# Stick-breaking attention on one core: masked entries zeroed by position on GpSimd, and the next pair's scores issued a pair ahead

## The chip, the cores and the metric

The kernel runs on 1 core of one Trainium2 chip. The metric is device time in microseconds (us) of one execution; lower is better. Engines are named as in the profile: PE is TensorE's matmul, PEld its weight load, DVE is VectorE, ACT is ScalarE, POOL is GpSimd, SP is SyncE.

## The reference

The program is a trunk of four residual layers over 256 tokens of width 1024. Layers 0 and 3 mix tokens by stick-breaking attention, layer 1 by latent attention, layer 2 by windowed attention; a SwiGLU block follows each. The change touches only stick-breaking, with 16 heads of 64:

```python
z = jnp.einsum('bqhd,bshd->bhqs', q_blk, k) * scale
valid = key_pos[None, :] < q_pos[:, None]
log_keep = jnp.where(valid, jax.nn.log_sigmoid(-z), 0.0)
log_keep_after = lax.cumsum(log_keep, axis=3, reverse=True) - log_keep
att = jnp.where(valid, jnp.exp(log_beta + log_keep_after), 0.0)
return jnp.einsum('bhqs,bshd->bqhd', att, v)
```

With softplus(z) = max(z, 0) + ln(1 + exp(-|z|)), log_keep is -softplus(z), and the exponent is z minus the sum of softplus over this key and all later valid keys. An entry is valid when its key comes before its query.

## The kernel before

Every engine has its own program, written out by hand in order, and engines meet at semaphores. Matrices are held as a high and a low part (float32r), so each product is three matmuls: high by high, high by low, low by high. The layer's 16 projection weights (units b to b+15, 128x2048 each) stream in by DMA; for each unit ACT makes the high part w_hi (L503, in `split`) and DVE the low part w_lo (L862, in `split`, counted by lo_done), some units ahead of PE's use.

Heads go in eight pairs p. `qk(p)` on PE projects a pair's queries and keys (24 matmuls for four of its eight k-tiles, so two halves); DVE scales them out of PSUM (L972, L974), ACT makes their high parts k_hi and q_hi (L565, L567), DVE the low parts (`qk_low`: L981, L985). `logits(p)` computes transposed scores, keys on partitions and queries on columns, into two PSUM banks: "early" are keys 0 to 127 for all queries of both heads (512 columns), "late" keys 128 to 255 for queries 128 to 255 (256 columns). Before the scores, two bf16 matmuls of an identity with a mask write -1e30 at the masked entries (L1459, L1461). ACT does |z|, exp and ln on the 768 columns (`soft`: L579, L581, L583); DVE adds max(z, 0) twice, into sp_hi and into a scratch buffer (L998), and sp_lo is their difference (L1003). `keep_sums(p)` accumulates minus the sums of softplus onto the scores (L1487 to L1489, waiting for softplus and then for sp_lo). ACT's exp (`weights`, L588) makes the attention weights, and `values(p)` (L1410, L1412) multiplies them with v. ACT and DVE split the result for the output projection (L592 o_hi, L948 o_lo).

In loop step p PE issues logits(p), the values of finished pairs (two pairs in steps 2, 4 and 6, one in step 7), the second half of qk(p+1) and the first of qk(p+2), then keep_sums(p). In steps 6 and 7 parts of the output projection stand in place of qk: `out_part(i, j, tiles)` needs o_lo of each of its tiles, and w_lo of unit b+12+j for its first tile. sp_hi and sp_lo (`soft_split`) exist once, not per pair; so do k_split and q_split. The scores of pair p lie in bank pair p mod 2.

Of the kernel before, what the change touches and what calls it, by code (L numbers as in the profile page):

```python
# [22 lines left out]
FP32 = mybir.dt.float32  # L23
# [6 lines left out]
P = 128  # L30
# [76 lines left out]
def trunk(nc, w, x_in, consts, gains, bv, final_rows, rel_rows, rel_scratch, out):  # L107
    ctx = ExitStack()
    with ctx:
# [29 lines left out]
        q_split = placed("q_split", [P, 2, 2, SEQ], FP32R, 4 * KT * SEQ)  # L139
# [95 lines left out]
        def head_blocks(v):  # L235
            return v.rearrange("p (h b q) -> p h b q", h=2, b=2)
# [54 lines left out]
        def signals(tag, names):  # L291
# [8 lines left out]
            signals("m0", "v_new qk_new q_zero k_hi q_hi k_lo q_lo z ln softplus sp_lo sums att av o_hi o_lo"),  # L300
# [4 lines left out]
            signals("m3", "v_new qk_new q_zero k_hi q_hi k_lo q_lo z ln softplus sp_lo sums att av o_hi o_lo"),  # L305
# [41 lines left out]
        def _(pool):  # L347
# [84 lines left out]
            def query_zeros(i):  # L432
# [6 lines left out]
                for h in range(2):  # L439
                    if h:  # L440
                        pool.wait_ge(mixer[i].q_zero, 1)
                    pool.memset(q_split[others(h), :, h, :].bitcast(FP32), 0.0).then_inc(mixer[i].q_zero, 1)
                pool.wait_ge(mixer[i].q_zero, 2)

# [23 lines left out]
            for i in range(DEPTH):  # L468
# [5 lines left out]
                if i % 3 == 0:  # L474
                    query_zeros(i)
                if i == 1:
# [10 lines left out]
        def _(act):  # L487
# [57 lines left out]
            def stick_breaking(i):  # L545
# [17 lines left out]
                def qk_hi(p):  # L563
                    act.wait_ge(m.qk_new, 2 * p + 2)
                    act.activation(k_split[:, 0, :], k_all[:, p, :], ACT.Copy).then_inc(m.k_hi, 1)  # L565
                    for h in range(2):
                        act.activation(q_split[own(h), 0, h, :], q_all[own(h), p, :], ACT.Copy).then_inc(m.q_hi, 1)  # L567
# [7 lines left out]
                def soft(p):  # L575

                    e, z = buf(0, 768), two_banks[p % 2][:, 0:768]
                    act.wait_ge(m.z, p + 1)
                    t = step(act.activation(e, z, ACT.Abs))  # L579
# [5 lines left out]
                def weights(p):  # L585

                    act.wait_ge(m.sums, p + 1)
                    act.activation(buf(2 + p % 2, 768), two_banks[p % 2][:, 0:768], ACT.Exp).then_inc(m.att, 1)  # L588
# [258 lines left out]
        def _(dve):  # L847
# [102 lines left out]
            def stick_breaking(i):  # L950
# [28 lines left out]
                def qk_low(p):  # L979
# [3 lines left out]
                    for h in range(2):  # L983
                        dve.wait_ge(m.q_hi, 2 * p + h + 1)
                        dve.tensor_tensor(q_split[own(h), 1, h, :], q_all[own(h), p, :],  # L985
                                          q_split[own(h), 0, h, :].bitcast(FP32), ALU.subtract).then_inc(m.q_lo, 1)
# [3 lines left out]
                if i == 0:  # L990

                    dve.wait_ge(lut_summed, 1)
                    dve.tensor_copy(rel_lut[:, :], bank[7][0:16, 0:192]).then_inc(lut_copied, 1)
                for p in range(KT):
                    split(b + 7 + p)
                    dve.wait_ge(m.ln, p + 1)
# [1034 lines left out]
```

## Time and profile before

| What | Value |
|---|---|
| Median of 3 runs | 1161.99 us (1161.47 to 1162.59) |
| Profiled execution, its own time | 1161.93 us |
| Span of the profiled execution | 1160.1 us |
| PE busy | 1148.3 us, 99% of the span |
| DVE, ACT, POOL busy | 804.5, 633.8, 276.0 us |
| Granted TensorE clock, mean | 0.998 |
| Loop over eight pairs, layer 0 and layer 3 | from 41 to 111 us and from 882 to 952 us |

The span is the stretch that the profiler sees; the execution's own time is 1.83 us longer. An engine's busy time is the union of its instructions' times; matmuls overlap one another, so the distance from one start to the next is what one costs in a dense run.

### The profile page before, as it was taken

The numbers are of one execution on the slowest core, as the hardware profiler recorded it, in microseconds if no ns is written. First come the engines' busy times: TensorE is split into PE (matmuls) and PEld (weight loads), VectorE is DVE, ScalarE is ACT, GpSimd is POOL, SyncE is SP. The second block draws the span as 40 slices with busy tenths as digits, with TensorE's granted clock in tenths as the row PEclk, the third lists the DMA queues.
The fourth block names the chain that finished last, engine by engine and source line by source line (L and its number), as shares of the span: only waits on it lengthen the run. The fifth ranks groups of instructions, "written<-read, shape, count | busy, mean of one in ns | idle before, by whom it ended". The sixth has DMA issues, their size and how long they took to land.

```text
span 1160.1 us, 17714 instructions
## 1 busy us (share of the span) xinstructions
PE 1148.3 (99%) x7182; PEld 1020.4 (88%) x7182; DVE 804.5 (69%) x881; ACT 633.8 (55%) x753; POOL 276.0 (24%) x257
## 2 busy tenths in 40 slices
PE   9999999999999999999999999999999999999997
PEld 7899888888998888888899888888889998888885
DVE  6786877776588677777658777777546868777742
ACT  6776565564445556555346656555436765655632
POOL 2100533231123444221111343221110005332100
PEclk9999999999999999999999999999999999999999
DMA  9432555565563255555554355555555326555550
GB/s 350 166 110 73 218 189 195 197 199 191 186 208 111 97 191 185 182 187 196 197 182 146 110 181 188 197 195 182 183 184 178 110 73 219 190 197 195 197 184 37
DMA packets 31227, 201.75 MB, mean 174 GB/s; under 512 B 3648, under 2 KB 4736, under 8 KB 7728
## 3 DMA queue, kind: packets, MB, share of 16 engines
q1 hardware_dynamic: 28800, 196.88, 47.9%
q10 hardware_dynamic: 2032, 3.07, 1.0%
q8 instruction: 57, 0.93, 0.3%
q0 software_dynamic: 320, 0.72, 0.3%
q14 instruction: 18, 0.15, 0.0%
HBM read 198.43 MB, written 1.25 MB: 172 GB/s over the span
## 4 chain that ended last, share of the span: by engine, by line
PE 94%; DVE 2%; POOL 1%; DMA 1%; SPq 1%; issue 1%; ACT 1%; ACTq 0%; DVEq 0%; POOLq 0%
PE banks L1338 41%; PE banks L1342 21%; PE banks L1326 8%; PE banks L1332 6%; PE banks L1334 6%; PE banks L1333 6%; PE banks L1473 1%; DMA raw<-w 1%; PE banks L1410 1%; PE banks L1487 1%; PE banks L1629 1%; PE banks L1475 0%; SPq L320 0%; PE banks L1641 0%; POOL scratch L360 0%
## 5 line engine op out<-in xcount | busy, mean ns | idle before, releaser
L862 DVE TENSOR_TENSOR w_lo<-raw,w_hi 128x2048 fp32r<-128x2048 f32 x180 | 442.7, 2464 | 191.8 <-ACT w_hi L503 191.6
L503 ACT ACTIVATE w_hi<-raw 128x2048 fp32r<-128x2048 f32 x183 | 348.6, 1907 | 61.6 <-PE banks L1326 21.1
L1338 PE MATMUL banks<-x_split,w_hi 128*128 128x512 f32 x1408 | 336.9, 391 | 0.0
L1338 PEld LDWEIGHTS banks<-x_split,w_hi 128*128 128x128 f32 x1408 | 258.4, 188 | 50.3 <-DVE w_lo L862 0.4
L1342 PEld LDWEIGHTS banks<-x_split,w_lo 128*128 128x128 f32 x1408 | 181.0, 191 | 7.1
L1342 PE MATMUL banks<-x_split,w_lo 128*128 128x256 f32 x1408 | 184.0, 283 | 0.0
L1338 PE MATMUL banks<-hid_split,w_hi 128*128 128x512 f32 x528 | 129.9, 391 | 0.0
L1338 PEld LDWEIGHTS banks<-hid_split,w_hi 128*128 128x128 f32 x528 | 95.6, 188 | 17.5
L1332 PE MATMUL banks<-x_split,w_hi 128*128 128x256 f32 x384 | 110.0, 286 | 0.0
L1333 PE MATMUL banks<-x_split,w_hi 128*128 128x256 f32 x384 | 108.6, 283 | 0.0
L1334 PE MATMUL banks<-x_split,w_lo 128*128 128x256 f32 x384 | 108.6, 283 | 0.0
L395 POOL TENSOR_TENSOR scratch<-scratch,rstd 128x512 f32<-128x512 f32 x44 | 57.2, 1300 | 196.1 <-ACT scratch L788 196.1
L398 POOL TENSOR_TENSOR scratch<-scratch 128x512 f32<-128x512 f32 x44 | 72.2, 1642 | 126.9 <-DVE scratch L1250 126.2
L515 ACT ACTIVATE x_split<-x,vec 128x256 fp32r<-128x256 f32 x64 | 31.6, 506 | 107.5 <-DVE x L1285 81.4
L776 ACT ACTIVATE scratch<-banks 128x512 f32<-128x512 f32 x44 | 26.2, 595 | 95.1 <-PE banks L1342 95.1
L1332 PEld LDWEIGHTS banks<-x_split,w_hi 128*128 128x128 f32 x384 | 73.4, 191 | 2.2 <-issue 1.0
L383 POOL TENSOR_TENSOR sq<-x 128x256 f32<-128x256 f32 x41 | 42.9, 1047 | 133.0 <-DVE x_split L887 131.8
L1342 PEld LDWEIGHTS banks<-hid_split,w_lo 128*128 128x128 f32 x528 | 70.5, 191 | 4.4
L1333 PEld LDWEIGHTS banks<-x_split,w_hi 128*128 128x128 f32 x384 | 73.5, 191 | 0.1
L1334 PEld LDWEIGHTS banks<-x_split,w_lo 128*128 128x128 f32 x384 | 73.5, 191 | 0.0
L1342 PE MATMUL banks<-hid_split,w_lo 128*128 128x256 f32 x528 | 71.7, 282 | 0.0
L383 POOL TENSOR_TENSOR sq_sum<-x 128x256 f32<-128x256 f32 x7 | 7.1, 1009 | 240.2 <-DVE x_split L887 240.2
(200 smaller groups left out, 1628.7 us busy)
## 6 DMA issues: line engine op xcount, KB each, us to landing
raw<-w SPq DMA_DIRECT2D x183, 1024.0 KB, 4.9
raw<-w SPq DMA_DIRECT2D x8, 256.0 KB, 6.4
x<-x_in SPq DMA_DIRECT2D x4, 256.0 KB, 5.3
raw<-w SPq DMA_DIRECT2D x2, 512.0 KB, 7.5
k_all<-k_all ACTq DMA_DIRECT2D x1, 960.0 KB, 8.0
rel_bias<-rel_scratch POOLq DMA_DIRECT2D x8, 64.0 KB, 3.0
y_gain<-final_rows ACTq DMA_DIRECT2D x1, 512.0 KB, 6.3
out<-y_rows SPq DMA_DIRECT2D x2, 256.0 KB, 2.6
```

The costliest lines, as they stand in the source:

```text
L383: step(pool.tensor_tensor(dst[:, :], x[:, k, :], x[:, k, :], ALU.mult))
L395: pool.tensor_tensor(gate, gate, both(rstd[:, 0:SEQ]), ALU.mult).then_inc(f.scaled, 1)
L398: pool.tensor_tensor(value, gate, value, ALU.mult).then_inc(f.hid, 1)
L503: act.activation(w_hi[u % HI_SLOTS][:, :], raw[slot][:, :], ACT.Copy).then_inc(hi_done, 1)
L515: act.activation(x_hi[:, k, :], x[:, k, :], ACT.Identity, scale=gain(n, k)).then_inc(norm.hi, 1)
L862: dve.tensor_tensor(w_lo[slot][:, :], raw[slot][:, :], w_hi[u % HI_SLOTS][:, :].bitcast(FP32), ALU.subtract).then_inc(lo_done, 1)
L1326: ins = pe.matmul(dst, a, v, start=first and n == 0, stop=last and n == 2, skip_group_check=True)
L1332: pe.matmul(dst, wh, xh, start=first, stop=False, skip_group_check=True)
L1333: pe.matmul(dst, wh, xl, start=False, stop=False, skip_group_check=True)
L1334: return pe.matmul(dst, wl, xh, start=False, stop=last, skip_group_check=True)
L1338: return pe.matmul(pair(b), wt[0], xs, start=first, stop=False, skip_group_check=True)
L1342: return pe.matmul(pair(b)[:, 1, :], wt[1], xs[:, 0, :], start=False, stop=last, skip_group_check=True)
```

## The change

The mask matmuls go, and the scores start their own accumulation. In their place POOL gets three instructions for each pair (`stick_masks`, L448): it writes zero at masked entries of the scratch copy of softplus and of sp_hi before they are summed (signal sp_kept), and of the attention weights before `values` (signal att_kept). An affine_select compares an index worked out from partition and column with zero and keeps or replaces the entry. So that one instruction reaches all four diagonal blocks, columns are laid out anew: late first (256 columns), then early by query block and head; q_split gets the same order.

PE's order changes too. logits(p+1) stands ahead of keep_sums(p), behind the first half of qk(p+2); it waits until `weights` of the pair two back has read its banks. The parts of the output projection in steps 5 to 7 are distributed anew. DVE and ACT follow with `softplus(p+1)`, `softplus_low(p+1)` and `soft(p+1)` in step p. Since sp_hi exists once, its second writing waits for the sums of the pair before.

```diff
+            def later_keys_out(v):
+                return pool.affine_select(v[:, 0:512], v[:, 0:512], [[0, 4], [1, P]], ALU.is_gt, 0.0, base=0,
+                                          channel_multiplier=-1)
+            def stick_masks(i):
+                def kept_softplus(p):
+                    pool.wait_ge(m.softplus, 2 * p + 1)
+                    later_keys_out(buf(1, 768)).then_inc(m.sp_kept, 1)
+                    pool.wait_ge(m.softplus, 2 * p + 2)
+                    later_keys_out(soft_split[:, 0, :]).then_inc(m.sp_kept, 1)
+                kept_softplus(0)
+                for p in range(KT):
+                    if p < KT - 1:
+                        kept_softplus(p + 1)
+                    pool.wait_ge(m.att, p + 1)
+                    later_keys_out(buf(2 + p % 2, 768)).then_inc(m.att_kept, 1)
...
+                soft(0)
+                qk_hi(1)
                 for p in range(KT):
-                    soft(p)
                     if p < KT - 1:
+                        soft(p + 1)
                         split(b + 8 + p)
-                        qk_hi(p + 1)
+                    if p < KT - 2:
+                        qk_hi(p + 2)
                     for done in finished(p):
                         out_hi(done)
                     weights(p)
...
+                def softplus(p):
+                    dve.wait_ge(m.ln, p + 1)
+                    for dst in (buf(1, 768), sp_hi):
+                        if p:
+                            dve.wait_ge(m.sums if dst is sp_hi else m.sp_lo, p)
+                        dve.scalar_tensor_tensor(dst, stick_scores(p), 0.0, buf(0, 768),
+                                                 ALU.max, ALU.add).then_inc(m.softplus, 1)
+                def softplus_low(p):
+                    dve.wait_ge(m.sp_kept, 2 * p + 2)
+                    dve.tensor_tensor(sp_lo, buf(1, 768), sp_hi.bitcast(FP32), ALU.subtract).then_inc(m.sp_lo, 1)
...
                 for p in range(KT):
                     split(b + 7 + p)
+                    if p < KT - 2:
+                        qk(p + 2)
+                    if p < KT - 1:
+                        softplus(p + 1)
+                    if p < KT - 2:
+                        qk_low(p + 2)
+                    if p < KT - 1:
+                        softplus_low(p + 1)
                     for done in finished(p):
                         dve.wait_ge(m.o_hi, done + 1)
                         out_lo(m, o_lo[:, done, :], bank[6 + done % 2][:, 0:SEQ], o_hi[:, done, :])
...
-                    mask = head_blocks(mask_b[:, 0:512])[:, :, 0, :]
-                    pe.matmul(head_blocks(early)[:, :, 0, :], ident_b[:, :], mask, start=True, stop=False,
-                              skip_group_check=True)
-                    pe.matmul(late, ident_b[:, :], mask, start=True, stop=False, skip_group_check=True)
+                    if p < 2:
+                        pe.wait_ge(m.v_new, 2 * p + 2)
+                    else:
+                        pe.wait_ge(m.att, p - 1)
...
+                logits(0)
+                qk(1, range(4, KT))
+                qk(2, range(0, 4))
                 for p in range(KT):
+                    if p < KT - 1:
+                        logits(p + 1)
+                    if p < KT - 2:
+                        qk(p + 2, range(4, KT))
+                    elif p == KT - 2:
+                        out_part(i, 1, range(0, 4))
+                    else:
+                        out_part(i, 0, range(4, 6))
+                        out_part(i, 1, range(4, 5))
                     for done in finished(p):
                         values(done)
+                    keep_sums(p)
+                    if p < KT - 3:
+                        qk(p + 3, range(0, 4))
+                    elif p == KT - 3:
                         out_part(i, 0, range(0, 4))
```

The changed program's line numbers differ: softplus is L1029, softplus_low L1034, qk_low L1010 and L1014, w_lo L891, o_lo L977, the sums L1533 to L1535, the scores L1519 and L1521. Three places show the new order.

First, DVE in layer 0 from step 6 on, where w_lo_57 is unit b+13 and w_lo_58 is b+14. Before:

```order
L862 TENSOR_TENSOR w_lo_57<-raw_52,w_hi 128x2048 [waits hi_done]
L998 SCALAR_TENSOR_TENSOR soft_split<-banks,scratch 128x768 [waits ln_m0]
L998 SCALAR_TENSOR_TENSOR scratch<-banks,scratch 128x768
L972 SCALAR_TENSOR_TENSOR q_all<-banks,rstd 128x256 [waits unit_used]
L974 TENSOR_TENSOR k_all<-banks,rstd 128x256
L1003 TENSOR_TENSOR soft_split<-scratch,soft_split 128x768 [waits softplus_m0]
L981 TENSOR_TENSOR k_split<-k_all,k_split 128x256 [waits k_hi_m0]
L985 TENSOR_TENSOR q_split<-q_all,q_split 64x256 [waits q_hi_m0] x2
L948 TENSOR_TENSOR o_split<-banks,o_split 128x256 [waits o_hi_m0] x2
L862 TENSOR_TENSOR w_lo_58<-raw_53,w_hi 128x2048 [waits hi_done]
```

Of the change, from the second softplus of step 5 on:

```order
L1029 SCALAR_TENSOR_TENSOR soft_split<-banks,scratch 128x768 [waits sums_m0]
L1010 TENSOR_TENSOR k_split<-k_all,k_split 128x256 [waits k_hi_m0]
L1014 TENSOR_TENSOR q_split<-q_all,q_split 64x2x128 [waits q_hi_m0] x2
L1034 TENSOR_TENSOR soft_split<-scratch,soft_split 128x768 [waits sp_kept_m0]
L891 TENSOR_TENSOR w_lo_57<-raw_52,w_hi 128x2048 [waits hi_done]
L1029 SCALAR_TENSOR_TENSOR scratch<-banks,scratch 128x768 [waits sp_lo_m0,ln_m0]
L1029 SCALAR_TENSOR_TENSOR soft_split<-banks,scratch 128x768 [waits sums_m0]
L1034 TENSOR_TENSOR soft_split<-scratch,soft_split 128x768 [waits sp_kept_m0]
L977 TENSOR_TENSOR o_split<-banks,o_split 128x256 [waits o_hi_m0] x2
L891 TENSOR_TENSOR w_lo_58<-raw_53,w_hi 128x2048 [waits hi_done]
```

The low parts o_lo of pairs 4 and 5 (L977) now stand behind a softplus that waits for PE's sums of pair 6, and behind a subtraction that waits for POOL.

Second, PE at the end of step 6, the sums of pair 6 and what follows. Before, the masks and scores of pair 7 follow:

```order
L1487 MATMUL banks<-soft_split,neg_sums 128x512 [waits sp_lo_m0]
L1488 MATMUL banks<-soft_split,neg_sums 128x256
L1489 MATMUL banks<-soft_split,neg_sums 128x2x128
L1459 MATMUL banks<-mask_b,ident_b 128x2x128
L1461 MATMUL banks<-mask_b,ident_b 128x256
L1473 MATMUL banks<-q_split,k_split 128x512 [waits k_hi_m0,q_hi_m0]
```

Of the change, where the scores of pair 7 have gone ahead, the output projection of tile 4 follows at once:

```order
L1533 MATMUL banks<-soft_split,neg_sums 128x512 [waits sp_lo_m0]
L1534 MATMUL banks<-soft_split,neg_sums 128x256
L1535 MATMUL banks<-soft_split,neg_sums 128x256
L1376 MATMUL banks<-o_split,w_hi 128x256 [waits o_lo_m0]
L1377 MATMUL banks<-o_split,w_hi 128x256
L1378 MATMUL banks<-o_split,w_lo_56 128x256
```

Its first matmul waits for o_lo of pair 4, which the DVE rows above place behind those same sums.

Third, POOL behind its two memsets of q_split in layer 0. Before, the squares for the next norm follow:

```order
L442 MEMSET q_split 64x2x256 [waits cast_done,ss_norm]
L442 MEMSET q_split 64x2x256 [waits q_zero_m0]
L383 TENSOR_TENSOR sq_sum<-x 128x256 [waits lo_norm,q_zero_m0]
L383 TENSOR_TENSOR sq<-x 128x256 [waits lo_norm,pool_step]
L387 TENSOR_TENSOR sq_sum<-sq_sum,sq 128x256 [waits pool_step]
```

Of the change:

```order
L443 MEMSET q_split 64x4x128 [waits cast_done,ss_norm]
L443 MEMSET q_split 64x4x128 [waits q_zero_m0]
L448 AFFINE_SELECT scratch<-scratch 128x512 [waits softplus_m0,q_zero_m0]
L448 AFFINE_SELECT soft_split<-soft_split 128x512 [waits softplus_m0]
L448 AFFINE_SELECT scratch<-scratch 128x512 [waits softplus_m0]
L448 AFFINE_SELECT soft_split<-soft_split 128x512 [waits softplus_m0]
L448 AFFINE_SELECT scratch<-scratch 128x512 [waits att_m0]
```

24 such instructions in each of the two layers now stand between the memsets and the squares.

## Rows read from the trace of the kernel before

**Rows 1.** The page: busy time of each engine, share of the span, instructions.

```profile
PE 1148.3 (99%) x7182; PEld 1020.4 (88%) x7182; DVE 804.5 (69%) x881; ACT 633.8 (55%) x753; POOL 276.0 (24%) x257
```

**Rows 2.** Waits of PE, longest: waited for, us, times, longest.

```profile
PE banks L1368 <- POOL ss L361: 1.4, 1, 1.4
```

**Rows 3.** Timeline of PE, layer 0, steps 0 and 1: start us, us, instruction.

```profile
48.64 0.48 PE L1487 MATMUL banks<-soft_split,neg_sums 128*128 128x512 f32 x1
48.97 0.28 PE L1488 MATMUL banks<-soft_split,neg_sums 128*128 128x256 f32 x1
...
49.20 0.28 PE L1459 MATMUL banks<-mask_b,ident_b 128*128 128x256 bf16 x1
...
49.79 0.40 PE L1473 MATMUL banks<-q_split,k_split 128*128 128x512 f32 x1
50.02 0.28 PE L1475 MATMUL banks<-q_split,k_split 128*128 128x256 f32 x1
```

**Rows 4.** Timeline of PE, end of the last sums of layer 0.

```profile
110.59 0.28 PE L1489 MATMUL banks<-soft_split,neg_sums 128*128 128x256 f32 x1
110.70 0.28 PE L1332 MATMUL banks<-o_split,w_hi 128*128 128x256 f32 x1
```

**Rows 5.** Timeline of ACT: step 4 of layer 0, and the last weights.

```profile
76.49 0.81 ACT L579 ACTIVATE scratch<-banks 128x768 f32<-128x768 f32 x1 [0.47 <-PE banks L1475]
...
78.96 1.90 ACT L503 ACTIVATE w_hi<-raw 128x2048 fp32r<-128x2048 f32 x1
81.86 0.42 ACT L565 ACTIVATE k_split<-k_all 128x256 fp32r<-128x256 f32 x1 [0.99 <-DVE k_all L974]
...
110.91 0.81 ACT L588 ACTIVATE scratch<-banks 128x768 f32<-128x768 f32 x1 [4.13 <-PE banks L1489]
```

**Rows 6.** Timeline of DVE: step 4 of layer 0, and one o_lo.

```profile
75.54 2.29 DVE L862 TENSOR_TENSOR w_lo<-raw,w_hi 128x2048 fp32r<-128x2048 f32 x1
79.09 0.96 DVE L998 SCALAR_TENSOR_TENSOR soft_split<-banks,scratch 128x768 fp32r<-128x768 f32 x1 [1.26 <-ACT scratch L583]
...
81.07 0.42 DVE L972 SCALAR_TENSOR_TENSOR q_all<-banks,rstd 128x256 f32<-128x256 f32 x1 [0.16 <-PE banks L1334]
...
81.74 0.95 DVE L1003 TENSOR_TENSOR soft_split<-scratch,soft_split 128x768 fp32r<-128x768 f32 x1
82.61 0.42 DVE L981 TENSOR_TENSOR k_split<-k_all,k_split 128x256 fp32r<-128x256 f32 x1
82.94 0.86 DVE L985 TENSOR_TENSOR q_split<-q_all,q_split 64x256 fp32r<-64x256 f32 x2
...
109.27 0.42 DVE L948 TENSOR_TENSOR o_split<-banks,o_split 128x256 fp32r<-128x256 f32 x1
```

**Rows 7.** Groups by line and shape, POOL: busy us, mean ns of one.

```profile
L452 POOL TENSOR_TENSOR scratch<-scratch,small 128x512 f32<-128x512 f32 x8 | 8.3, 1041 | 43.4 <-DVE small L1178 43.4
...
L367 POOL CAST mask_b<-scratch 128x832 bf16<-128x832 f32 x1 | 0.9, 872 | 0.0
L365 POOL CAST ident_b<-table 128x128 bf16<-128x128 f32 x1 | 0.3, 287 | 0.0
```

**Rows 8.** Timeline of POOL, squares after layer 0, and a product in the SwiGLU block.

```profile
120.95 2.54 POOL L383 TENSOR_TENSOR sq<-x 128x256 f32<-128x256 f32 x1
...
126.02 0.61 POOL L383 TENSOR_TENSOR sq<-x 128x256 f32<-128x256 f32 x1
...
185.09 1.29 POOL L398 TENSOR_TENSOR scratch<-scratch 128x512 f32<-128x512 f32 x1 [3.50 <-DVE scratch L1250]
```

**Rows 9.** Timeline of DVE at the same two places.

```profile
120.32 2.70 DVE L862 TENSOR_TENSOR w_lo<-raw,w_hi 128x2048 fp32r<-128x2048 f32 x1
...
185.50 3.02 DVE L862 TENSOR_TENSOR w_lo<-raw,w_hi 128x2048 fp32r<-128x2048 f32 x1 [0.56 <-ACT w_hi L503]
```

**Rows 10.** Stretches at the end: busy us (count) of PE, PEld, DVE, ACT, POOL, PEclk, DMA.

```profile
1152.00:1154.00 2.00, 0.47 (x3) 0.04 (x1) 0.75 (x1) 1.48 (x4) 0.00 (x0) 1.00 0.18 68
1154.00:1156.00 2.00, 0.00 (x0) 0.00 (x0) 1.32 (x7) 0.92 (x4) 0.00 (x0) 0.76 0.52 195
```

More of the change, by code:

```diff
@@ L299, in trunk @@
         mixer = [
-            signals("m0", "v_new qk_new q_zero k_hi q_hi k_lo q_lo z ln softplus sp_lo sums att av o_hi o_lo"),
+            signals("m0", "v_new qk_new q_zero k_hi q_hi k_lo q_lo z ln softplus sp_kept sp_lo sums att att_kept av o_hi o_lo"),
             signals("m1", "q_part q_new rope_tab rot_in krope_sum krope_new kfill k_part k_new v_part v_new logits max_new "
@@ L304, in trunk @@
                           "o_hi o_lo"),
-            signals("m3", "v_new qk_new q_zero k_hi q_hi k_lo q_lo z ln softplus sp_lo sums att av o_hi o_lo"),
+            signals("m3", "v_new qk_new q_zero k_hi q_hi k_lo q_lo z ln softplus sp_kept sp_lo sums att att_kept av o_hi o_lo"),
         ]
@@ L475, in _ @@
                     query_zeros(i)
+                    stick_masks(i)
                 if i == 1:
@@ L566, in qk_hi @@
                     for h in range(2):
-                        act.activation(q_split[own(h), 0, h, :], q_all[own(h), p, :], ACT.Copy).then_inc(m.q_hi, 1)
+                        act.activation(q_split[own(h), 0, :, h, :], q_all[own(h), p, :].rearrange("p (b q) -> p b q", b=2),
+                                       ACT.Copy).then_inc(m.q_hi, 1)
                 qk_hi(0)
@@ L587, in weights @@
                     act.wait_ge(m.sums, p + 1)
-                    act.activation(buf(2 + p % 2, 768), two_banks[p % 2][:, 0:768], ACT.Exp).then_inc(m.att, 1)
+                    act.activation(buf(2 + p % 2, 768), stick_scores(p), ACT.Exp).then_inc(m.att, 1)
                 def out_hi(p):
@@ L1471, in logits @@
                             pe.wait_ge(m.k_hi, p + 1)
-                        kk, qq = k_split[:, key_low, :], q_split[:, query_low, :, :]
-                        pe.matmul(early, kk[:, 0:P], qq.rearrange("p h s -> p (h s)"), start=False, stop=query_low == 1,
+                        kk, qq = k_split[:, key_low, :], q_split[:, query_low, :, :, :]
+                        first = not (key_low or query_low)
+                        pe.matmul(early, kk[:, 0:P], qq.rearrange("p b h q -> p (b h q)"), start=first, stop=query_low == 1,
                                   skip_group_check=True)
-                        last = pe.matmul(late, kk[:, P:SEQ], qq[:, :, P:SEQ], start=False, stop=query_low == 1,
-                                         skip_group_check=True)
+                        last = pe.matmul(late, kk[:, P:SEQ], qq[:, 1, :, :].rearrange("p h q -> p (h q)"), start=first,
+                                         stop=query_low == 1, skip_group_check=True)
                     last.then_inc(m.z, 1)
@@ L1483, in keep_sums @@
                         pe.wait_ge(neg_tri_done, 1)
-                    for low, done, count in ((0, m.softplus, 2 * p + 2), (1, m.sp_lo, p + 1)):
+                    for low, done, count in ((0, m.sp_kept, 2 * p + 2), (1, m.sp_lo, p + 1)):
                         pe.wait_ge(done, count)
                         sp = soft_split[:, low, :]
-                        pe.matmul(early, neg_tri, sp[:, 0:512], start=False, stop=False, skip_group_check=True)
-                        pe.matmul(late, neg_tri, sp[:, 512:768], start=False, stop=low == 1, skip_group_check=True)
-                        last = pe.matmul(head_blocks(early)[:, :, 1, :], neg_one, sp[:, 512:768], start=False,
+                        pe.matmul(early, neg_tri, sp[:, 256:768], start=False, stop=False, skip_group_check=True)
+                        pe.matmul(late, neg_tri, sp[:, 0:256], start=False, stop=low == 1, skip_group_check=True)
+                        last = pe.matmul(early[:, 256:512], neg_one, sp[:, 0:256], start=False,
                                          stop=low == 1, skip_group_check=True)
```

54 lines of the change are left out of this document (21 added, 33 removed).

## The prediction

> **What bounds the kernel now.** The page comes first: PE is busy 99% of the span, DVE 69%, ACT 55%, POOL 24% [rows 1]. So time is won only where PE has less to issue or waits less, and any new wait of PE costs its full length unless a wait already there swallows it. The waits of PE come next: the longest in the whole span is 1.4 us, near the start, outside the attention loop [rows 2]. The timeline of PE then gives the price of everything in the loop: a 256-column matmul starts 0.12 us after the one before [rows 4], a 512-column one takes 0.23 [rows 3]. One small wait recurs: the second L1487 starts its successor 0.33 later instead of 0.23, because sp_lo is just late [rows 3]. That is 0.10 us, in the four pairs per layer (0, 1, 3, 5) whose steps have no values to cover it.
>
> **What the change takes away.** The two masks and the first pair of score matmuls take 49.20 to 49.79, 0.59 us, of which the scores are 0.23 + 0.12 [rows 3, 4]; the masks are 0.24. Eight pairs give 1.92 us in each layer. The four sp_lo waits go as well, since a pair's scores now run a whole step ahead of its sums: 0.40. Gain: 2.3 us per layer, 4.6 in all. The new columns change no size of a PE instruction, so they are costed at nothing.
>
> **What it adds on PE's path.** A step without values takes PE 1.05 (three score groups of 0.35) + 48 x 0.12 + 0.94 (sums) = 7.75 us. I follow DVE from the moment at which PE has issued the last of sums(p-1), t = 0. An engine sees PE's signal 0.21 us after issue [rows 4, 5]; I take 0.1 between other engines and 0.15 to PE, estimates of the same order. DVE's occupancies are 0.67 for scaling a pair's q and k, 0.87 for each softplus and for sp_lo, 0.33 for k_lo, 0.43 for each half of q_lo, 2.29 for w_lo [rows 6].
>
> A select's own price is not in the trace. The nearest rows are one-input POOL casts: 128 columns take 0.287 us and 832 take 0.872, so 512 come to 0.61 [rows 7]. A product of the same 512 columns with two inputs takes 1.04, my upper bound; the lower one is 0.50, a little under the cast line. I take 0.65.
>
> The trace also shows that POOL and DVE take turns. A POOL square of 0.61 us took 2.54 when it began during a w_lo, and a w_lo of 2.29 took 3.02 when it began 0.41 us into a POOL product of 1.29 [rows 6, 8, 9]. Both instructions read two SBUF tensors there. On the other side 0.61 is unhindered beside DVE work out of PSUM [rows 8]. So k_lo, q_lo, sp_lo and w_lo should take turns with the selects, softplus should not. The Trainium skill (GPSIMD Engine Reference, Key points) says that GpSimd shares its SBUF interfaces with VectorE and contends with instructions of two SBUF inputs; the rows agree, and by that sentence the selects meet those four DVE instructions. Whether a one-input select also holds DVE up no row shows; I take that it does, for 0.5 us (0.65 less what POOL spends before it reads, about 0.15: the square above ended 0.47 after w_lo did, against 0.61 alone).
>
> Then, in a step whose predecessor had no values: qk(p+1) ended 0.94 before t = 0, so DVE scales it from -0.73 to -0.06, writes the first softplus to 0.82, the second to 1.70 (it needs the sums, there at 0.21), k_lo to 2.03. Now the select of sp_hi holds it to 2.53, half of q_lo to 2.96, the select of the weights to 3.46, the other half to 3.89; PE sees q_lo at 4.05. PE wants it behind 24 projections and two score groups, at 2.88 + 0.70 = 3.58. **PE waits 0.47**, in scores 2, 3, 5 and 7: 1.9 us. After a step with values DVE has done its first softplus early and is in time.
>
> **Scores 1**: measured from the end of scores 0, DVE gets qk(1) at 2.88 + 0.21, and does the scaling (3.76), two softplus (5.51), k_lo (5.84), a select's turn (6.34) and q_lo (7.20). PE wants q_lo at 5.76 + 0.70 = 6.46 and sees it at 7.35: 0.9 us.
>
> **Step 6, unit b+13.** From t = 0 at the sums of pair 5, DVE has q_lo at 3.89, sp_lo at 4.77, and only then does the w_lo that the moved `out_part(i, 1, ...)` needs: 7.06, at PE 7.2. PE stands there at 3.58 + 0.47 + 0.35 = 4.4. It waits 2.8 us. Before, that projection came a step later.
>
> **Step 7, o_lo.** This is the largest. Behind the sums of pair 6 PE has nothing to issue but `out_part(i, 0, range(4, 6))`, which needs o_lo of pair 4. On DVE that stands behind the softplus of pair 7, whose second half needs those very sums: 0.21 + 0.95 + 0.1 + 0.65 (select) + 0.1 + 0.87 (sp_lo) + 0.42 (o_lo) + 0.15 = 3.45 us of idle PE.
>
> **Values 7.** Exp and select now follow the last sums: 0.21 + 0.81 + 0.1 + 0.65 + 0.15 = 1.92 us [rows 5], against 12 projections, 1.44: 0.5. Without a select it was 1.17, and covered.
>
> ACT is tight but in time. From the scores' end its chain is 0.21 + 2.5 for the three passes (76.49 to 78.96), 1.9 for w_hi, 1.2 for k_hi and two halves of q_hi (three of 0.4), 0.81 for the weights that free the banks, 0.15 to PE; with 1.05 for the scores that is 7.8 against 7.75 [rows 5]. I count nothing: a wait of 0.1 would run beside the one for q_lo.
>
> **Sum.** Per layer 1.9 + 0.9 + 2.8 + 3.45 + 0.5 = 9.5, less 2.3, is +7.2 us; two layers +14.4. The profiled execution's own time is 1161.93 (span 1160.1 and 1.83 around it), the median 1161.99, so no shift is needed: **1176.3 us**.
>
> **Rivals.** *POOL gives way*: a one-input select waits for DVE but never holds it. Then scores 2 to 7 don't wait, scores 1 wait 0.4, w_lo of b+13 comes at 6.8 for a PE at 3.93 (2.9), the rest stays: 7.2 - 2.3 = 4.9 per layer, 1171.7 us. Without any meeting of the two, w_lo comes at 6.2, 2.3 late: 1170.5. For it: no row has a one-input POOL instruction first; against it: the w_lo of 3.02.
>
> *Slow selects*: at 1.04 us each turn is 0.9, and the first select ends 0.3 after DVE wants k_lo. The four waits of 0.47 become 1.6, scores 4 and 6 wait 0.6, scores 1 1.4, step 7 and the last values 0.4 more each: 16.5 - 2.3 = 14.2 per layer, about 1190 us. The skill's page above (Performance pitfalls) gives 1.03 to 2.03 cycles an element for a compare and select, at 1.2 GHz 0.44 to 0.87 us; by 0.87 the sum would be an estimated 1185, by 0.44 about 1171.
>
> *Faster*: if DVE reached w_lo of b+13 and o_lo of pair 4 before PE needs them, only the gain of 4.6 would be left, 1157.3 us. This is decided at 2.3 us of waits per layer; step 7 alone, without its select, is 2.8. It takes a DVE order other than the one shown, or hand-overs far shorter than the 0.21 seen. *No change*: waits that happen to sum to 2.3 per layer, 1162.
>
> *The clock*: PE's last stretch with matmuls ends within 1152 to 1154, and the mean granted clock of 1154 to 1156 is 0.76, on its way from 2.4 to 1.2 GHz [rows 10]; the idle of 1.4 us in [rows 2] left the mean at 0.998. An idle of 3.45 us may therefore drop it. Matmuls then take twice the time for a while, an estimated 1 to 3 us per layer. It comes on top of the first three; I leave it out of the forecast and in the range.
>
> **How the numbers follow.** Turns with selects near 0.65: 45%. POOL gives way or no meeting: 25%. Slow selects: 17%. Faster: 8%. Within 0.2%, about what a measurement of this kernel can tell from no change: 3%. Slower still: 2%. The range runs from 1167 (shorter selects, no turns, with 1 us per layer less of tail) to 1192 (slow selects with some clock lost), leaving out the faster and equal cases and the dearest end. Faster 0.08, same 0.03, slower 0.89.
>
> **What would show it.** L1459 and L1461 gone, PE's count down by 32 matmuls. PE idle after L1535 of pair 6 by 3 to 4 us, ended by DVE's o_lo (L977), in both layers; before the `out_part` of step 6 by 2 to 3 us, ended by w_lo (L891). Affine selects of about 0.65 us, and q_lo stretched where one runs beside it. Wrong would be: no idle at those two places, selects over 1 us (dearer), or scores that wait for `weights` (ACT) instead of q_lo.

## The result, and the profile after

The changed kernel takes 1179.38 us (median of 4, 1178.64 to 1180.87) against 1162.29 us (1161.47 to 1163.25) for the kernel before on the same chip: a ratio of 1.0149, 95% interval 1.0137 to 1.0161, so 1.5% slower. The forecast was 1176.3 us, in a range from 1167 to 1192. The profiled execution took 1180.87 us, its span is 1179.1 us, and the mean granted clock 0.991 where it had been 0.998.

The page's row of busy times and the clock's row of 40 slices, to lay beside [rows 1]. The last line is the clock's row of the kernel before:

```profile
PE 1153.7 (98%) x7150; PEld 1024.6 (87%) x7150; DVE 814.8 (69%) x881; ACT 631.9 (54%) x753; POOL 308.6 (26%) x305
...
PEclk9998999999999999999999999999999989999999
...
PEclk9999999999999999999999999999999999999999
```

PE has 32 matmuls fewer: the masks are gone. POOL has 48 instructions more. PE is nevertheless busy 5 us longer, and the clock row has an 8 in the two slices in which the attention loops end. The waits of PE in the changed kernel (waited for, total us, times, longest), to lay beside [rows 2]:

```profile
PE banks L1376 <- DVE o_split L977: 7.0, 2, 3.5
PE banks L1376 <- DVE w_lo L891: 5.2, 2, 2.6
...
PE banks L1519 <- DVE q_split L1014: 1.1, 2, 0.5
...
PE banks L1454 <- POOL scratch L448: 0.5, 2, 0.3
```

All four are new, each twice: once per layer. The two on top are o_lo of pair 4 (step 7) and w_lo of unit b+13 (step 6). Because the ends of matmuls overlap, I read the length of an idle from starts: the distance from one matmul's start to the next, less what the first one costs. PE's timeline in layer 0 shows scores 1, scores 2, the two idles, and the last values:

```profile
48.22 0.28 PE L1521 MATMUL banks<-q_split,k_split 128*128 128x256 f32 x1
49.04 0.50 PE L1519 MATMUL banks<-q_split,k_split 128*128 128x512 f32 x1 [0.54 <-DVE q_split L1014]
49.38 0.28 PE L1521 MATMUL banks<-q_split,k_split 128*128 128x256 f32 x1
...
56.77 0.28 PE L1521 MATMUL banks<-q_split,k_split 128*128 128x256 f32 x1
56.99 0.50 PE L1519 MATMUL banks<-q_split,k_split 128*128 128x512 f32 x1
...
100.07 0.28 PE L1521 MATMUL banks<-q_split,k_split 128*128 128x256 f32 x1
102.93 0.58 PE L1376 MATMUL banks<-o_split,w_hi 128*128 128x256 f32 x1 [2.58 <-DVE w_lo L891]
...
107.38 0.44 PE L1454 MATMUL banks<-scratch,v_all 128*64 128x256 f32 x2
...
109.80 0.28 PE L1535 MATMUL banks<-soft_split,neg_sums 128*128 128x256 f32 x1
113.57 0.58 PE L1376 MATMUL banks<-o_split,w_hi 128*128 128x256 f32 x1 [3.48 <-DVE o_split L977]
113.94 0.42 PE L1377 MATMUL banks<-o_split,w_hi 128*128 128x256 f32 x1
114.16 0.42 PE L1378 MATMUL banks<-o_split,w_lo 128*128 128x256 f32 x1
...
121.79 0.28 PE L1378 MATMUL banks<-o_split,w_lo 128*128 128x256 f32 x1
122.34 0.44 PE L1454 MATMUL banks<-scratch,v_all 128*64 128x256 f32 x2 [0.27 <-POOL scratch L448]
```

A 256-column matmul costs 0.12 from start to start, so the idles are 2.86 - 0.12 = 2.74 us and 3.77 - 0.12 = 3.65 us; scores 1 wait 0.82 - 0.12 = 0.70, scores 2 wait 0.10, the last values 0.43. Here a 512-column matmul that started after a wait also delayed its successor by 0.34 instead of 0.24 (49.04 to 49.38): 0.10 more each time, called the restart below. Behind the second idle matmuls start 0.22 apart instead of 0.12. That is the clock, as the stretches show (us, then busy us and count of PE, PEld, DVE, ACT, POOL, granted clock, DMA; the last two are from layer 3):

```profile
103.00:106.00 3.00, 3.00 (x14) 3.00 (x15) 0.94 (x1) 1.75 (x1) 0.63 (x1) 0.50 0.00 0
...
110.00:113.00 3.00, 0.08 (x1) 0.00 (x0) 2.14 (x2) 0.81 (x1) 1.22 (x2) 0.99 0.00 0
113.00:119.00 6.00, 5.43 (x26) 4.71 (x26) 3.04 (x4) 0.00 (x0) 0.00 (x0) 0.50 0.01 3
...
953.00:957.00 4.00, 2.64 (x22) 2.64 (x23) 2.27 (x2) 3.15 (x3) 0.64 (x1) 1.00 0.00 0
...
964.00:970.00 6.00, 6.00 (x29) 5.04 (x29) 2.31 (x2) 0.39 (x1) 0.00 (x0) 0.53 0.00 0
```

Both idles of layer 0 are followed by a stretch at 0.50, 1.2 GHz instead of 2.4. In layer 3 only the second one is (964 to 970 at 0.53); 953 to 957, behind the first, is at 1.00.

POOL's selects, by shape (busy us, mean ns of one):

```profile
L448 POOL TENSOR_SCALAR_AFFINE_SELECT scratch<-scratch 128x512 f32<-128x512 f32 x32 | 21.0, 657 | 142.6 <-DVE scratch L1029 123.1 <-ACT scratch L614 18.6
L448 POOL TENSOR_SCALAR_AFFINE_SELECT soft_split<-soft_split 128x512 fp32r<-128x512 f32 x16 | 11.9, 742 | 19.1 <-DVE soft_split L1029 19.1
```

DVE and POOL in step 7, between the last matmul of the sums and o_lo, then DVE at q_lo of pair 3, in step 1:

```profile
110.12 0.96 DVE L1029 SCALAR_TENSOR_TENSOR soft_split<-banks,scratch 128x768 fp32r<-128x768 f32 x1 [6.18 <-PE banks L1535]
111.15 0.64 POOL L448 TENSOR_SCALAR_AFFINE_SELECT soft_split<-soft_split 128x512 fp32r<-128x512 f32 x1 [6.50 <-DVE soft_split L1029]
111.73 0.64 POOL L448 TENSOR_SCALAR_AFFINE_SELECT scratch<-scratch 128x512 f32<-128x512 f32 x1
111.82 1.36 DVE L1034 TENSOR_TENSOR soft_split<-scratch,soft_split 128x768 fp32r<-128x768 f32 x1 [0.74 <-POOL soft_split L448]
113.10 0.41 DVE L977 TENSOR_TENSOR o_split<-banks,o_split 128x256 fp32r<-128x256 f32 x1
...
63.25 1.64 DVE L1014 TENSOR_TENSOR q_split<-q_all,q_split 64x256 fp32r<-64x256 f32 x2
```

Rows one, two, four and five are the chain of the 3.65 us: softplus, its select, sp_lo, o_lo. The sp_lo (L1034), 0.96 elsewhere, takes 1.36 because the select of the weights (row three) began 0.09 ahead of it; the two q_lo (L1014), 0.86 together in [rows 6], take 1.64 beside two selects.

### The profile page after: what moved, and what is told of

Same layout as the page of the kernel before. It is cut to its first block, busy times and chain, and to the rows that moved or that the text cites. A ratio compares the mean times of both kernels' runs of the same rounds, so it can differ in the third digit from the quotient of the medians.

```text
span 1179.1 us, 17729 instructions
## 1 busy us (share of the span) xinstructions
PE 1153.7 (98%) x7150; PEld 1024.6 (87%) x7150; DVE 814.8 (69%) x881; ACT 631.9 (54%) x753; POOL 308.6 (26%) x305
## 3 DMA queue, kind: packets, MB, share of 16 engines
q10 hardware_dynamic: 2032, 3.07, 1.0%
## 4 chain that ended last, share of the span: by engine, by line
PE 90%; DVE 5%; ACT 1%; POOL 1%; issue 1%; DMA 1%; SPq 1%; ACTq 0%; DVEq 0%; POOLq 0%
PE banks L1382 40%; PE banks L1386 21%; PE banks L1370 7%; PE banks L1376 5%; PE banks L1377 5%; PE banks L1378 5%; DVE w_lo L891 1%; PE banks L1519 1%; PE banks L1454 1%; DMA raw<-w 1%; PE banks L1533 1%; PE banks L1679 1%; PE banks L1706 1%; PE banks L1691 1%; DVE q_split L1014 0%
## 5 line engine op out<-in xcount | busy, mean ns | idle before, releaser
L891 DVE TENSOR_TENSOR w_lo<-raw,w_hi 128x2048 fp32r<-128x2048 f32 x180 | 441.8, 2458 | 188.2 <-ACT w_hi L526 188.2
L1376 PE MATMUL banks<-o_split,w_hi 128*128 128x256 f32 x192 | 58.8, 306 | 12.4 <-DVE o_split L977 7.0
```

What stands on the lines that cost most here:

```text
L891: dve.tensor_tensor(w_lo[slot][:, :], raw[slot][:, :], w_hi[u % HI_SLOTS][:, :].bitcast(FP32), ALU.subtract).then_inc(lo_done, 1)
L1376: pe.matmul(dst, wh, xh, start=first, stop=False, skip_group_check=True)
```

## The experiments

Each ran on one chip together with the kernel before; ratios are against that kernel, and runs from different chips are compared by them. "By starts" means read as above, from the starts of PE's matmuls. Theory A is the prediction's: PE waits at two places of the tail for late DVE results, and those idles halve the clock for a while. Theory B: the selects and their turns with DVE are the main cost, wherever the waits appear.

**1. PE's order in the tail.**

```diff
-                    elif p == KT - 2:
-                        out_part(i, 1, range(0, 4))
-                    else:
+                    elif p == KT - 1:
                         out_part(i, 0, range(4, 6))
...
                     keep_sums(p)
...
+                    elif p == KT - 2:
+                        out_part(i, 1, range(0, 4))
```

> The four projections of rows 0 to 3 of the second output unit (24 matmuls, 2.88 us) stand behind the sums of pair 6 instead of ahead of the values of pairs 4 and 5; nothing else is changed. Theory A (PE stands idle at two places of the tail because what it issues next needs a late DVE result, and these idles also halve the clock for a while): the values and sums now run while w_lo of unit b+13 is made, and the projections while o_lo of pair 4 is made. By the times of the changed kernel PE waits about 1.2 us for w_lo and about 1.2 us for o_lo, not 2.74 and 3.65, which is 4.0 us less in each layer, 8 in both; idles of 1.2 us should leave the clock at 2.4 GHz, as the 1.4 us wait of the kernel before did, which is another 5 to 7 us. Expected 1165 us, between 1163 and 1168. Theory B (the selects on POOL and their turns with DVE are the main cost, wherever PE's order puts the wait): at most the clock comes back, 1172 us or more.

Measured: 1164.23 us, ratio 1.0018 (1.0009 to 1.0028). Some 15 of the 17 us are gone by moving 24 matmuls in each of the two layers. PE's waits in this run:

```profile
PE banks L1376 <- DVE o_split L977: 1.7, 2, 0.9
...
PE banks L1519 <- DVE q_split L1014: 1.1, 2, 0.5
...
PE banks L1454 <- POOL scratch L448: 0.5, 2, 0.3
```

The wait for w_lo is gone from the list, and 0.1 us by starts, where 1.2 had been expected. That 1.2 is the old 2.74 less the 1.5 us that the values of two pairs take; the sums of pair 6, another 1.0 us, now stand ahead of the moved projections too. Of the wait for o_lo 1.0 us is left per layer by starts. Theory A holds and B falls: the selects are all still there, and the time is far under B's 1172 us.

**2. o_lo early.** On ACT and DVE, PE untouched:

```diff
                         soft(p + 1)
+                        if p == KT - 2:
+                            for done in finished(p):
+                                out_hi(done)
                         split(b + 8 + p)
...
                     for dst in (buf(1, 768), sp_hi):
+                        if p == KT - 1 and dst is sp_hi:
+                            for done in finished(KT - 2):
+                                low_out(done)
...
```

> ACT writes o_hi of pairs 4 and 5 ahead of splitting a weight unit in step 6, and DVE writes their o_lo ahead of the second softplus of pair 7, which is the one that waits for the sums of pair 6. PE's order is that of the changed kernel. Theory A: the idle of 3.65 us in step 7 goes (about 0.3 us stays in front of the low half of the sums of pair 7), the idle of 2.74 us in step 6 stays, and so does its part of the low clock. That is 6.7 us less in both layers and 4 to 6 us of clock: expected 1168 us, between 1166 and 1171. Theory B: the second softplus, select and sp_lo of pair 7 still have to be done before its sums, so the wait only moves there and the time stays above 1175 us.

Measured: 1172.09 us, ratio 1.0086 (1.0070 to 1.0103), 1 us above the expected range. The wait for o_lo is gone, but a new one came in step 7, in front of the values of pair 6:

```profile
PE banks L1387 <- DVE w_lo L895: 5.1, 2, 2.6
PE banks L1465 <- POOL scratch L448: 2.9, 4, 1.2
```

The first line is the old idle of step 6, which this run keeps. On ACT the weight unit (1.9 us) now starts behind o_hi, at 109.31, and the weights of pair 6 stand behind it at 111.12, though the last matmul of their sums starts at 109.85; their select then takes 1.33 in turns with sp_lo and w_lo. PE waits 1.34 us there by starts in layer 0, and the list has this wait in both layers. That is the miss. The mechanism is A's: what DVE had queued ahead of o_lo set the idle, and a queue on another engine sets the next one.

**3. Narrow selects.**

```diff
-                return pool.affine_select(v[:, 0:512], v[:, 0:512], [[0, 4], [1, P]], ALU.is_gt, 0.0, base=0,
+                return pool.affine_select(v[:, 0:16], v[:, 0:16], [[0, 4], [1, 4]], ALU.is_gt, 0.0, base=0,
```

> Each of the 24 selects of a layer works on 16 of its 512 columns, so most masked entries are not zeroed; every instruction, order and wait of the changed kernel stays. Theory A: the four small waits of the scores go (0.2 each), that of scores 1 falls by 0.4, w_lo of b+13 comes two turns (0.8) earlier, the wait of step 7 loses a select of 0.5 and a turn of 0.4, that of the last values its 0.43: 3.4 us per layer, 6.8 in all and up to 2 us of clock: 1172 us, between 1169 and 1174, still about 10 us above the kernel before. Theory B: with the selects nearly free the time falls to that of the kernel before or under it, 1158 to 1164 us.

Measured: 1170.43 us, ratio 1.0075 (1.0059 to 1.0092): inside A's range. The idles of the tail are 2.18 and 2.82 us by starts, scores 1 wait 0.26 instead of 0.70, the other waits of the scores and that of the last values are gone, and the two q_lo of pair 3 take what they took in the kernel before:

```profile
62.48 0.87 DVE L1014 TENSOR_TENSOR q_split<-q_all,q_split 64x256 fp32r<-64x256 f32 x2
```

So in the order given the length of the selects is worth about half of the loss; with full selects and a better order the first experiment got lower still.

**4. Work in the idles, to keep the clock.**

```diff
+                def busy(n):
+                    for _ in range(n):
+                        pe.matmul(bank[4][:, 0:SEQ].rearrange("p (b q) -> p b q", b=2), k_split[others(0), 0, 0:P],
+                                  q_split[others(0), 0, :, 0, :], start=False, stop=False, skip_group_check=True)
...
+                        busy(19)
                         out_part(i, 1, range(0, 4))
                     else:
+                        busy(26)
                         out_part(i, 0, range(4, 6))
```

> PE issues 19 matmuls of 256 columns more in the idle of step 6 (2.3 of the 2.74 us) and 26 in that of step 7 (3.1 of 3.65 us); they add exact zeros to an accumulation that is open anyway, and wait for nothing. The late results stay as late. Theory A: the granted clock stays at 2.4 GHz behind both places and only the clock part comes back, 4 to 7 us: 1174 us, between 1172 and 1176. If the low clock behind the idles costs nothing (the matmuls there would wait anyhow): 1179 us. If it is most of the loss: under 1170 us.

Measured: 1175.20 us, ratio 1.0112 (1.0095 to 1.0129), against 1.0149 of the change, and inside the range expected. PE issues 90 matmuls more and the kernel is 0.37% faster, about 4.3 us (some 2 to 7 by the two intervals). The two stretches that were at 0.50 in the changed kernel, in this run:

```profile
103.00:106.00 3.00, 2.88 (x24) 2.67 (x23) 2.30 (x2) 2.97 (x3) 0.52 (x1) 1.00 0.00 0
...
113.00:119.00 6.00, 5.80 (x46) 5.08 (x46) 3.55 (x5) 1.20 (x2) 0.07 (x1) 1.00 0.00 0
```

The two traces also price the clock directly: the same matmuls, from the first projection behind an idle to values that come after, can be timed in both. This run, layer 0:

```profile
104.40 0.39 PE L1376 MATMUL banks<-o_split,w_hi 128*128 128x256 f32 x1
...
107.46 0.44 PE L1454 MATMUL banks<-scratch,v_all 128*64 128x256 f32 x2
...
113.65 0.38 PE L1376 MATMUL banks<-o_split,w_hi 128*128 128x256 f32 x1 [0.20 <-DVE o_split L977]
...
119.71 0.44 PE L1454 MATMUL banks<-scratch,v_all 128*64 128x256 f32 x2 [0.26 <-POOL scratch L448]
```

The stretch behind step 6's idle takes 3.06 us here and 4.45 in the changed kernel (102.93 to 107.38); from step 7's idle to the last values it is 6.06 and 8.77 (113.57 to 122.34). In layer 3 the two are 3.07 and 3.06, and 6.06 and 8.73. So in the changed kernel's profiled execution the clock cost 1.39 + 2.71 + 2.67 = 6.8 us. Its other three executions, with mean clocks of 0.993 and 0.994 instead of 0.991, were 0.9 to 2.2 us shorter.

**5. The gain alone.** The kernel before without L1459 and L1461:

```diff
-                    pe.matmul(head_blocks(early)[:, :, 0, :], ident_b[:, :], mask, start=True, stop=False,
-                              skip_group_check=True)
-                    pe.matmul(late, ident_b[:, :], mask, start=True, stop=False, skip_group_check=True)
...
-                        pe.matmul(early, kk[:, 0:P], qq.rearrange("p h s -> p (h s)"), start=False, stop=query_low == 1,
+                        pe.matmul(early, kk[:, 0:P], qq.rearrange("p h s -> p (h s)"), start=not (key_low or query_low), stop=query_low == 1,
...
```

> The kernel before with its 16 mask products per layer taken out and nothing else (masked entries are then not masked; the first score matmuls start the accumulation). It measures the gain by itself. If a mask product costs PE its issue (0.12 us, 32 in all): 3.84 us less, 1158.0 us against 1161.8. If what waits behind the scores (the low half of softplus, the weights) only waits longer, less than half of that: above 1160 us.

Measured: 1159.22 us against 1161.86, ratio 0.9970 (0.9959 to 0.9981): 2.2 to 4.8 us by the interval, which holds the 3.84 expected. The medians, 2.6 us apart, fall on executions of different granted clock, 0.997 and 0.998; those at 0.998 or more have medians of 1157.83 and 1161.79, 4.0 apart, and the two profiled executions differ by 4.1 (1157.83 and 1161.93). The late sp_lo of [rows 3] is still there in this run's sums (the successors start 0.30 to 0.32 behind it instead of 0.24), while in the changed kernel they start 0.23 to 0.24 behind it. Those four delays come to 0.3 us per layer, so the change had some 4.1 + 0.7 = 4.8 us to win.

**6. The tail, all of it.** On top of the first:

```diff
...
                     weights(p)
+                    if p == KT - 2:
+                        split(b + 8 + p)
...
+                        if p == KT - 1 and dst is sp_hi:
+                            for done in finished(KT - 2):
+                                low_out(done)
...
-                values(KT - 1)
                 out_part(i, 1, range(6, 7))
-                rest_high(i, 4, range(0, 5))
+                values(KT - 1)
+                rest_high(i, 4, range(0, 7))
...
```

> On top of the moved projections of the first experiment: ACT writes o_hi of pairs 4 and 5 and the weights of pair 6 ahead of the weight unit of step 6, DVE writes o_lo of pairs 4 and 5 ahead of the second softplus of pair 7, and the values of pair 7 stand behind one more group of six projections (two more tiles of the last rows' products cover o_lo behind them). Theory A: the waits that the first experiment left in the tail, 1.0 us for o_lo and 0.43 before the last values in each layer, go: 1161.4 us, between 1160.3 and 1162.5, level with the kernel before. Theory B (selects and turns): they only move; 1163.5 us or more.

Measured: 1161.91 us, ratio 1.0002 (0.9993 to 1.0011), as A expected. What is left of the waits eats the gain: in layer 0, by starts, 0.70 in scores 1, 0.1 in scores 2, 3, 5 and 7, the restarts behind these five, and 0.6 for a w_lo behind the attention.

**7 and 8. k_lo and q_lo between the two softplus.** The same edit on DVE, on the run above and on the changed kernel:

```diff
                     for dst in (buf(1, 768), sp_hi):
+                        if dst is sp_hi and p < KT - 1:
+                            qk_low(p + 1)
                         if p:
                             dve.wait_ge(m.sums if dst is sp_hi else m.sp_lo, p)
...
```

> The tail of the run named tail, and in every step DVE makes k_lo and q_lo between the two softplus of the pair before, so that they stand ahead of the one that waits for the sums, and ahead of its select. Theory A: the waits of the scores go as well (0.70 in scores 1 and about 0.2 in four others, per layer), and all of the 4.6 us of gain is left: 1158.3 us, between 1157 and 1160, faster than both kernels. Theory B (the turns with POOL hold DVE as long wherever k_lo and q_lo stand): no better than the run named tail.

> The changed kernel with only DVE's order altered: k_lo and q_lo between the two softplus, tail as it was. Theory A: scores 1 give back 0.70 us and four other scores 0.2 each, per layer, and the two long waits of the tail stay: 1176.4 us, between 1174 and 1178. If q_lo behind the softplus that waits for the sums is what paces the whole step and with it the tail: 1172 us or less. Theory B: no change, 1179 us.

Measured: 1165.82 us, ratio 1.0031 (1.0021 to 1.0042), and 1185.69 us, ratio 1.0207 (1.0192 to 1.0223). Both are worse than without the edit, by 4 and by 6 us; A had expected a gain and B at best none, and neither had a loss of this size. The waits of the scores did go; in their place PE waits for w_lo, here in the changed kernel with the edit:

```profile
PE banks L1375 <- DVE w_lo L891: 10.1, 6, 4.2
```

DVE's timeline in that run, in two of its steps, shows where DVE stands:

```profile
71.56 1.29 DVE L1014 TENSOR_TENSOR q_split<-q_all,q_split 64x256 fp32r<-64x256 f32 x2
72.88 0.96 DVE L1031 SCALAR_TENSOR_TENSOR soft_split<-banks,scratch 128x768 fp32r<-128x768 f32 x1
74.58 1.36 DVE L1036 TENSOR_TENSOR soft_split<-scratch,soft_split 128x768 fp32r<-128x768 f32 x1 [0.74 <-POOL soft_split L448]
...
79.39 0.94 DVE L1031 SCALAR_TENSOR_TENSOR scratch<-banks,scratch 128x768 f32<-128x768 f32 x1
80.26 0.41 DVE L1010 TENSOR_TENSOR k_split<-k_all,k_split 128x256 fp32r<-128x256 f32 x1
80.59 1.29 DVE L1014 TENSOR_TENSOR q_split<-q_all,q_split 64x256 fp32r<-64x256 f32 x2
```

Nothing but sp_lo is left behind the second softplus, so DVE stands still for the whole select (0.74) and then meets the next select in sp_lo. In the changed kernel k_lo and q_lo ran beside that select. Theory C, formed here: DVE with the selects on its path needs more time for a step than PE, and has become the engine that paces.

**9. Only the start.** On top of run 6, w_lo of unit b+7 ahead of scaling pair 1, and the edit of 7 for pair 0 alone:

```diff
+                split(b + 7)
                 qk(1)
                 softplus(0)
-                qk_low(1)
                 softplus_low(0)
                 for p in range(KT):
-                    split(b + 7 + p)
+                    if p:
+                        split(b + 7 + p)
...
+                        if p == 0 and dst is sp_hi:
+                            qk_low(1)
...
```

> The run named tail, with DVE's order altered at the loop's start alone: w_lo of unit b+7 is made while DVE is idle ahead of scaling pair 1, and k_lo and q_lo of pair 1 stand between the two softplus of pair 0. All later steps keep the changed kernel's order, in which the select of sp_hi runs beside k_lo and q_lo. Theory A: the wait of 0.70 us in scores 1 goes in both layers: 1160.5 us, between 1159.7 and 1161.3. Theory C (DVE is now the engine that paces every step, so work moved at the start only comes back as a wait for w_lo later): 1161.9 us.

Measured: 1160.23 us, ratio 0.9983 (0.9974 to 0.9992): faster than both kernels, by 1.9 us against the one before, and as A expected. The wait of scores 1 is gone. DVE had 4.5 us of idle in front of scaling pair 1, and the w_lo (2.29 us) fits into it, so C does not hold at the start.

**10. The last w_lo.** On run 9, in the two layers, the first split behind the attention moves into ACT's and DVE's idle, the third ahead of `add(4)`:

```diff
+                if i % 3 == 0:
+                    split(u + LEAD)
                 for t in range(4):
                     add(t)
...
                 norm_lo(n, 3)
+                if i % 3 == 0:
+                    split(u + LEAD + 2)
                 add(4)
...
```

> The run before this one, and the wait of 0.6 us for w_lo that the tail left behind the attention: ACT and DVE split the first weight unit of the output projection's successors while they are idle in the last step, and DVE the third one two tiles earlier. Theory A: 1.0 us less in the two layers, 1159.5 us, between 1158.7 and 1160.5, faster than both kernels. Theory C: no change against the run before this one.

Measured: 1161.60 us, ratio 0.9995 (0.9986 to 1.0004): no better than run 9, and 1.1 us above A's range, a miss. The wait for w_lo there gave way to waits for the low half of the normalised tiles, which DVE now makes later:

```profile
PE banks L1402 <- DVE x_split L920: 1.4, 4, 0.5
```

**11. Theory C.** Run 8 with the narrow selects of run 3.

> The run in which only k_lo and q_lo moved between the softplus (1185.7 us), with selects of 16 columns (most masked entries not zeroed). There DVE stood idle 0.74 us in each step for the select of sp_hi, and its turns cost 0.4 in q_lo and 0.4 in sp_lo. Theory C (this order puts the whole select on DVE's path, and DVE with it takes 8.4 us a step, more than PE's 7.75): with short selects DVE takes about 7.2 us, the steps are PE's again, the waits for w_lo in the steps go and the one of step 6 falls from 4.3 us to about 2; 1169 us, between 1167 and 1172, level with or under the changed kernel with short selects (1170.4). If the order itself is what costs (ACT later, or q_lo too early): 1177 us or more.

Measured: 1174.02 us, ratio 1.0098 (1.0083 to 1.0114), 2 us above the range. The waits for w_lo within the steps are gone, as C says; only the one of step 6 is left, 2.90 us by starts against 2.18 in run 3, where C expected about 2. DVE still stands 0.32 for the short select, and 0.21 for ACT's k_hi. What the edit costs is the distance to the same kernel without it: with full selects 0.58% (run 8 against the change), with short ones 0.23% (this run against run 3), whose intervals touch. As far as these ratios go, the full select on DVE's path is some 0.35 of the 0.58%, and the order itself looks a little worse than the one it replaced. How that rest divides into waits and clock (0.993 and 0.995 in the two profiles) was not separated.

## Why the prediction was right

**What the change takes away** was forecast at 4.6 us, 3.84 for the masks and 0.8 for the late sp_lo. Run 5 gives 2.2 to 4.8 for the masks alone, the profiles 4.1; the starts give 0.7 for sp_lo. The 1.4 us called the longest wait before is the second longest; the longest, 1.5 us (L1320), lies in the first 6 us of the span, so nothing in the sum rests on it.

**PE waits 0.47**, in scores 2, 3, 5 and 7: at the place and for the reason given, but it cost 0.21 each, 0.10 to 0.11 of waiting and 0.10 for the restart, which the sum did not have. The term that was mis-sized is the turn: 0.5 us was taken, and q_lo's pair shows (1.64 - 0.86) / 2 = 0.39. Two turns shorter by 0.11 take 0.22 off the wait; the hand-over to PE, 0.05 where 0.15 was taken, takes off most of the rest. That a one-input select holds DVE up, for which there was no row, is shown by these rows and by run 3; *POOL gives way* is out. So is *Slow selects*: 0.64 us is the usual duration, against 0.65 taken.

**Scores 1** was forecast at 0.9, and is 0.70 and 0.10 for the restart. **Step 6, unit b+13** was 2.8, and is 2.74: with the shorter turns both PE and w_lo were there some 0.3 earlier than in the sum. **Step 7, o_lo** was 3.45, and is 3.65. The hand-over from the sums was as taken: 0.20 from 109.92, when PE has issued the last of them (0.12 behind 109.80), to 110.12. But sp_lo took 0.4 more, for a turn with the select of the weights that the sum did not have, and the other three hand-overs, 0.07, 0.03 and 0.06 for the 0.1, 0.1 and 0.15 taken, gave back half of that. **Values 7** was 0.5, and is 0.43. Together 8.5 per layer for 9.5.

**The clock** was left out of the sum, and this is what the forecast lacked. Run 4 gives it 4.3 us in both layers by medians. Against run 4's trace the changed kernel's profiled execution lost 6.8 to it, 4.1 in layer 0 and 2.7 in layer 3, where the rival had 1 to 3 per layer. The waits come to 16.9 in both layers (4 x 0.21 + 0.80 + 2.74 + 3.65 + 0.43 = 8.46, twice). The profiled executions differ by 1180.87 - 1161.93 = 18.9 us; waits of 16.9 and a clock of 6.8 leave 4.8 for the gain, as run 5 and sp_lo say. Restarts behind the two long idles, some tenths in all, are not counted. By medians the loss is 17.1, and the forecast's 14.4 was too low by 2.7: the waits were 1 us per layer too dear, and this covered about half of the clock that was missing. That these two errors partly offset each other is luck; the places and the causes of the waits are not.

*Faster* came true only in another order. What decided, as the prediction said, was what DVE has queued ahead of w_lo and o_lo when PE comes to need them: run 1 shows it by moving PE's need, run 2 by moving o_lo up in DVE's queue, and run 9 reaches 1160.2, not 1157.3.

## What to carry to other kernels

Before work is moved ahead on the engine that bounds, list for each of its next instructions what the engine that feeds it still has queued in front: here 24 matmuls per layer in the wrong place cost 15 of 17 us, and in the better order of run 6 the same 48 selects left the kernel level with the one before. An idle of some microseconds on TensorE can cost more than its length (here 6.8 us of clock on top of 16.9 of waits), so independent work belongs there first. A helper on another engine needs work of the engine that waits for it beside it: moving that work away, to help one wait, left DVE standing for the select in every step of run 8.

## What was not expected of the hardware

The same idle left the clock in one execution and dropped it in another. Ahead of layer 0's loop PE is idle for about 1.5 us in both of these profiles, first the kernel before, then run 1:

```profile
30.00:33.00 3.00, 1.56 (x12) 1.33 (x12) 1.64 (x1) 1.37 (x1) 3.00 (x3) 1.00 0.91 307
33.00:36.00 3.00, 3.00 (x28) 3.00 (x27) 2.17 (x5) 0.84 (x2) 1.32 (x3) 1.00 0.28 117
```

```profile
30.00:33.00 3.00, 1.54 (x13) 1.31 (x11) 1.45 (x1) 1.91 (x1) 3.00 (x3) 1.00 0.95 327
33.00:36.00 3.00, 3.00 (x17) 3.00 (x17) 2.32 (x6) 0.84 (x2) 1.14 (x3) 0.58 0.22 93
```

Behind it one ran on at 2.4 GHz and issued 28 matmuls in 3 us, the other was at 1.2 GHz for most of them and issued 17; the changed kernel, whose program up to there is that of run 1, ran on at 2.4 GHz in its own profile. The clock fell there in the profiles of runs 4 and 7 too (0.52 and 0.55), and those of runs 1 and 7 are among the longer executions of their kernels: 1165.2 us with a fastest of 1163.5, and 1166.9 with 1165.0. In run 4 PE starts the last matmul of scores 7 at 101.54, in the changed kernel at 100.07, with the same instructions up to there: the drop ahead of the loop is worth some 1.5 us. Nor did the idle of step 6 drop the clock in layer 3, as it did in layer 0. Turns went both ways: a select that began 0.09 us ahead of a subtraction delayed it by 0.40, and a select that began beside k_lo took 0.76 instead of 0.64.
